# Down chunks in two halves between gate chunks, and weight loads of two chunks at a time, in a mixture-of-experts layer

## The chip, the cores and the metric

One core of one Trainium2 chip. The time is device microseconds of one execution. A core has TensorE (PE in the profile; PEld its weight loads), VectorE (DVE), ScalarE (ACT), GpSimd (POOL) and SyncE (SP). SyncE, ScalarE and GpSimd issue transfers, which run on 16 DMA engines. The kernel moves 450 MB, nearly all of it expert weights in float32.

## The reference, cut to what matters

512 tokens of width 1024 pass a layer with attention and a convolution, then a mixture of 32 experts, of which each token takes four. The expert part is what the change is about:

```python
def expert_block(args):
    tok, g, e = args
    xb = xf[tok]
    hu = xb @ w_gate_up[e] + b_gate_up[e]
    a = jnp.minimum(hu[:, :D_FF], SWIGLU_LIMIT)
    lin = jnp.clip(hu[:, D_FF:], -SWIGLU_LIMIT, SWIGLU_LIMIT)
    act = a * jax.nn.sigmoid(SWIGLU_ALPHA * a) * (lin + 1)
    return (act @ w_down[e] + b_down[e]) * g[:, None].astype(xb.dtype)
```

Here w_gate_up is (32, 1024, 2048) and w_down (32, 1024, 1024).

## The kernel before

The first 260 us compute the layer up to the router. Then the experts follow one after the other; one expert with up to 96 of its tokens is a job. Were an expert chosen by more than 96 tokens, further rounds of 32 jobs would follow; the number of jobs is read from memory (`bodies`, line 377). Jobs 0 and 1 are written out, and the rest is a hardware loop on each engine, with one job per pass.

A job's weights are 12 chunks of 1 MB, each 128 partitions by 8 KB: eight gate chunks (w_gate_up) and four down chunks (w_down). The chunks are numbered in the order in which PE uses them. `gu_chunk` (line 313) and `dn_chunk` (317) give the numbers, and `raw_slot` (298) gives the place in SBUF: 12 slots, chunk m in slot m % 12. Chunks 7 and 8 go to a place of their own once (`place`, 307). Before the change the twelve numbers of a job run: eight gates of expert j, then the four downs of expert j - 1.

SyncE issues the loads in this order (`job`, line 477), all on one queue. Each waits until the chunk 12 before it is used (`wait_slot`, 448): w_used counts the chunks that PE has finished, and chunk m waits for m - 11. Each slot has a semaphore w_loaded, on which PE waits ahead of the chunk.

On PE (`rest_of_job`, 1884, and `head`, 1873) a pass of the loop takes gates 4 to 7 of job j, the four downs of expert j - 1, and gates 0 to 3 of job j + 1. `gate_up` (1823) is 12 matmuls of 512 columns, four at a time side by side in the array; each is two instructions, with a weight load each. `down` (1834) is 24 matmuls of 256 columns in the same manner. So a gate chunk has 24 matmul instructions, a down chunk 48 of half the length. The gates of all jobs add up in the same banks gu_bank; gate 0 of the next job waits until VectorE has taken the sums (gu_taken) and has the next tokens ready (x_gained). The first down waits for the transposed activations (aT_ready) and for the down sums before it to be taken (y_taken).

On VectorE a job (`job`, 1529) takes the gate sums with the biases (lines 1461, 1462), clamps them (1465, 1466), transposes the gathered tokens of the next job (1472) and multiplies by the gain (1478), gates (1485, 1490, with ScalarE's sigmoid between), transposes the activations into aT (1498; chunk by chunk, each when its down chunk of the expert before is done), and takes the down sums (1511 to 1517). GpSimd gathers the tokens of the next job once x_turned tells that their place is free (line 651), and scatters the results, scaled by ScalarE, with addition into sum_rows (661). ScalarE loads the biases.

At the end PE takes the last expert's four downs by themselves, the last expert's rows are added by a matmul, and the final norm follows.

## Time and profile before

| | |
|---|---|
| Median of 3 runs (lowest, highest) | 1281.37 us (1281.32, 1281.72) |
| The profiled execution | 1282.38 us |
| Its span in the profile | 1280.6 us |
| Experts' part, from the first gate chunk | 262 to 1263 us |
| PE busy in the span | 1265.1 us |
| Moved by DMA | 450.31 MB |

The profile is of one execution. Busy time is the time in which an engine had an instruction at work; for PE the ends of matmuls are modelled. Times in the rows below are microseconds from the span's start, durations of one instruction in ns where three values stand with slashes (least, median, most). "Idle before" is followed by what ended it; "issue" means that the profile shows nothing for which the engine waited. In the chain, a piece is the stretch by which the end was advanced, not the whole length of an instruction. A DMA share is the busy share of the 16 engines; it can come out a little over 1.

### The profile page before, as it was taken

Reading aid. Unit: us, or ns where it says so; the run is one execution under the profiler, and the core shown is the slowest. Engines: PE = TensorE matmul, PEld = TensorE weight load, DVE = VectorE, ACT = ScalarE, POOL = GpSimd, SP = SyncE. Lnnn points to the kernel's source line nnn. Section 1 sums busy time; section 2 is a strip of 40 time slices with the busy share of each in tenths; the row PEclk is TensorE's granted clock in tenths of the full one; section 3 lists DMA queues with packets and bytes.
Section 4 is the critical chain, followed back from the end, with each engine's and each line's share of the span. In section 5 each row is a group of like instructions: output and inputs, shape, how many; then the busy total and the mean of one; then the engine's idle time right before and its main releaser. Section 6 shows DMA issues by size and latency. Waiting matters only on the chain.

```text
span 1280.6 us, 32819 instructions
## 1 busy us (share of the span) xinstructions
PE 1265.1 (99%) x13814; PEld 846.1 (66%) x13814; DVE 585.0 (46%) x984; ACT 184.2 (14%) x279; POOL 317.4 (25%) x319
## 2 busy tenths in 40 slices
PE   8999999999999999999999999999999999999997
PEld 7867777844676766766666556656576666667664
DVE  7776666555433333333333333333333333444345
ACT  4243443410000000000000000000000000000002
POOL 2035533011333332222222222222222222222220
PEclk9999999999999999999999999999999999999999
DMA  9222117589999999999999999999999999999994
GB/s 261 73 66 66 66 67 269 237 325 406 411 414 413 410 419 418 417 420 412 412 416 414 414 416 421 416 419 418 422 420 416 419 418 416 419 418 416 417 398 169
DMA packets 95377, 450.31 MB, mean 352 GB/s; under 512 B 12208, under 2 KB 37280, under 8 KB 45936
## 3 DMA queue, kind: packets, MB, share of 16 engines
q1 hardware_dynamic: 84288, 430.47, 82.2%
q0 software_dynamic: 9568, 18.97, 5.7%
q10 hardware_dynamic: 1488, 0.40, 0.1%
q8 instruction: 24, 0.39, 0.1%
q14 instruction: 9, 0.07, 0.0%
HBM read 439.54 MB, written 18.67 MB: 358 GB/s over the span
## 4 chain that ended last, share of the span: by engine, by line
PE 96%; DVE 2%; ACT 1%; DMA 1%; issue 0%; DVEq 0%; SPq 0%; ACTq 0%
PE gu_bank L1830 50%; PE bank L1844 21%; PE bank L1847 5%; PE bank L1597 5%; PE bank L1599 4%; PE bank L1598 4%; PE first_gu_bank L1830 2%; PE bank L1681 1%; PE bank L1695 1%; PE bank L1658 1%; DMA x_sb<-in_x_dram 1%; PE bank L1806 1%; DVE probs_a L1192 0%; PE fin_bank L1915 0%; PE bank L1615 0%
## 5 line engine op out<-in xcount | busy, mean ns | idle before, releaser
L1830 PE MATMUL gu_bank<-raw,xT 128*32 128x512 f32 x2976 | 331.7, 592 | 0.0
L1830 PEld LDWEIGHTS gu_bank<-raw,xT 128*32 128x32 f32 x2976 | 189.4, 110 | 130.4 <-issue 39.6
L1461 DVE TENSOR_TENSOR gate_in<-gu_bank,b_gu 128x768 f32<-128x768 f32 x31 | 29.7, 958 | 528.6 <-PE gu_bank L1830 528.6
L651 POOL DMA_INDIRECT x_got<-xn_rows,gather_list x96 | 114.5, 1193 | 341.7 <-DVE xT L1472 308.4
L1830 PE MATMUL gu_bank<-raw_c,xT 128*32 128x512 f32 x1488 | 172.1, 592 | 0.0
L1844 PE MATMUL bank<-raw_a,aT 128*32 128x256 f32 x2232 | 170.5, 379 | 0.0
L1847 PE MATMUL bank<-raw_a,aT 128*32 128x256 f32 x744 | 165.6, 379 | 0.0
L1844 PEld LDWEIGHTS bank<-raw_a,aT 128*32 128x32 f32 x2232 | 119.8, 110 | 36.5 <-issue 2.8
L1830 PEld LDWEIGHTS gu_bank<-raw_c,xT 128*32 128x32 f32 x1488 | 94.9, 110 | 65.2 <-issue 19.8
L937 ACT ACTIVATE sig_in<-gate_in 128x768 f32<-128x768 f32 x32 | 27.0, 845 | 641.0 <-DVE gate_in L1465 615.9
L1844 PE MATMUL bank<-raw_b,aT 128*32 128x256 f32 x1152 | 98.4, 380 | 0.0
L1847 PE MATMUL bank<-raw_b,aT 128*32 128x256 f32 x384 | 93.0, 380 | 0.1
L1830 PE MATMUL gu_bank<-raw_e,xT 128*32 128x512 f32 x744 | 92.3, 592 | 0.0
L1844 PE MATMUL bank<-raw_d,aT 128*32 128x256 f32 x1116 | 90.2, 379 | 0.0
L661 POOL DMA_INDIRECT sum_rows<-y_out,scatter_list x31 | 46.6, 1503 | 174.0 <-ACT y_out L945 114.2
L1830 PE MATMUL gu_bank<-raw_b,xT 128*32 128x512 f32 x720 | 89.5, 592 | 0.0
L1498 DVE STREAM_TRANSPOSE aT<-lin_in 128x192 f32<-128x192 f32 x128 | 63.6, 521 | 53.7 <-PE bank L1847 52.4
L1847 PEld LDWEIGHTS bank<-raw_a,aT 128*32 128x32 f32 x744 | 81.8, 110 | 7.1 <-issue 0.2
L1847 PE MATMUL bank<-raw_d,aT 128*32 128x256 f32 x372 | 85.3, 379 | 0.0
L945 ACT ACTIVATE y_out<-y_out,scatter_list 96x768 f32<-96x768 f32 (+1 forms) x62 | 44.8, 723 | 279.9 <-DVE y_out L1514 269.3
L1844 PEld LDWEIGHTS bank<-raw_b,aT 128*32 128x32 f32 x1152 | 62.0, 110 | 20.5 <-issue 6.0
L1844 PEld LDWEIGHTS bank<-raw_d,aT 128*32 128x32 f32 x1116 | 60.0, 110 | 15.0
(285 smaller groups left out, 1667.2 us busy)
## 6 DMA issues: line engine op xcount, KB each, us to landing
raw<-in_w_gate_up_dram SPq DMA_DIRECT2D x128, 1024.0 KB
raw_c<-in_w_gate_up_dram SPq DMA_DIRECT2D x62, 1024.0 KB
raw_a<-in_w_down_dram SPq DMA_DIRECT2D x62, 1024.0 KB
raw_b<-in_w_down_dram SPq DMA_DIRECT2D x32, 1024.0 KB
raw_e<-in_w_gate_up_dram SPq DMA_DIRECT2D x31, 1024.0 KB
raw_d<-in_w_down_dram SPq DMA_DIRECT2D x31, 1024.0 KB
raw_b<-in_w_gate_up_dram SPq DMA_DIRECT2D x30, 1024.0 KB
raw<-in_w_in_dram SPq DMA_DIRECT2D x24, 512.0 KB, 6.1
```

The source lines that it names most:

```text
L651: pool.indirect_dma_start(out=x_got[:, r, :], out_offset=None, in_=xn_quarters, in_offset=bass.IndirectOffsetOnAxis(ap=gather_list[:, r:r ...
L661: pool.indirect_dma_start(out=sum_rows, in_=y_out[0:TILE, :], in_offset=None, out_offset=bass.IndirectOffsetOnAxis(ap=scatter_list[0:TILE, ...
L937: act.activation(sig_in[:, :, :], gate_in[:, :, :], ACT.Sigmoid, scale=ALPHA).then_inc(sig_ready, 1)
L945: ins = act.activation(y_out[0:TILE, cols], y_out[0:TILE, cols], ACT.Copy, scale=scatter_list[0:TILE, 1:2].bitcast(F32))
L1461: dve.tensor_tensor(gate_in[:, :, :], gu[:, :, 0:QUARTER], gate_b, ALU.add)
L1498: dve.transpose(aT[:, 2 * i:2 * i + 2, :].rearrange("p k (r t) -> p k r t", r=GROUPS), lin_in[:, :, :].rearrange("p r (f k) -> p k r f", k ...
L1597: pe.matmul(dst, a_hi, b_hi, start=start, stop=False)
L1598: pe.matmul(dst, a_hi, b_lo, start=False, stop=False)
L1599: return pe.matmul(dst, a_lo, b_hi, start=False, stop=stop)
L1830: ins = pe.matmul(gu[c * GROUP:(c + 1) * GROUP, r, :], x[:, i, r * GROUP:(r + 1) * GROUP], w[:, c], start=first, stop=last)
L1844: pe.matmul(bank_[c * GROUP:(c + 1) * GROUP, cols], aT[:, k, c * GROUP:(c + 1) * GROUP], w[:, at:at + QUARTER], start=first and r % 2 == 0 ...
L1847: ins = pe.matmul(bank_[TILE:P, cols], aT[:, k, r * GROUP:(r + 1) * GROUP], w[:, at:at + QUARTER], start=first and r % 2 == 0, stop=last a ...
```

## The change

On PE the four downs stand in two halves: gates 4 and 5, downs 0 and 1, gates 6 and 7, downs 2 and 3, then gates 0 to 3 of the next job. The numbers of the chunks follow that (GU_AT, DN_AT). In the last job all four gates come first, then the four downs, while the numbers and SyncE's order stay as in the others.

The slots are ordered so that five times two of them lie side by side. SyncE loads ten of the twelve chunks of a job two at a time, 16 KB a partition with one semaphore; the source is contiguous for each partition. The load waits until both slots are free, and PE waits for it ahead of the first of the two alone. Job 0 and the four downs of the last expert are loaded one by one, and so are gates 0 and 1 of each job (slots 8 and 9).

On VectorE the clamps now follow the transpose and the gain of the next job's tokens. The last job is written out without that transpose and gain.

```diff
         def raw_slot(m):
 
-            for ring in (raw01, raw_a, raw_d, raw_b, raw_e, raw_c):
+            return raw_slots(m, 1)
+
+        def raw_slots(m, n):
+
+            for ring in (raw01, raw_a, raw_b, raw_d, raw_e, raw_c):
                 if m < ring.shape[1]:
-                    return ring[:, m, :]
+                    return ring[:, m:m + n, :].rearrange("p two n -> p (two n)")
                 m -= ring.shape[1]
 
-        ONCE = 7
+        TWO_AT = (0, 2, 4, 6, 10)
+
+        def starts_two(m):
+            return m >= RAW and m % RAW in TWO_AT
+
+        def ends_two(m):
+            return m >= RAW and m % RAW - 1 in TWO_AT
+
+        ONCE = 6
+        HEAD = GU_CHUNKS // 2
...
+        GU_AT, DN_AT = (0, 1, 2, 3, 4, 5, 8, 9), (6, 7, 10, 11)
+
         def gu_chunk(n, i):
 
-            return i if n == 0 else n * JOB - DN_CHUNKS + i
+            return i if n == 0 else n * JOB - DN_CHUNKS + GU_AT[i]
 
         def dn_chunk(n, i):
 
-            return n * JOB + 2 * GU_CHUNKS + i
+            return (n + 1) * JOB - DN_CHUNKS + DN_AT[i]
...
             def load_gu(e, i, m, b, turns):
-                wait_slot(m, b, turns)
-                sp.dma_start(place(m), w_gate_up[0, e].rearrange("(p i) n -> i p n", i=GU_CHUNKS)[i])\
+                if ends_two(m):
+                    return
+                n = 2 if starts_two(m) else 1
+                wait_slot(m + n - 1, b, turns)
+                sp.dma_start(raw_slots(m % RAW, n) if m >= RAW else place(m),
+                             w_gate_up[0, e].rearrange("(p i) n -> p (i n)", p=P)[:, i * CHUNK:(i + n) * CHUNK])\
                   .then_inc(w_loaded[m % RAW], 16)
 
-            def load_dn(e, i, m, b, turns):
-                wait_slot(m, b, turns)
-                sp.dma_start(raw_slot(m % RAW),
-                             w_down[0, e].rearrange("(p i h) n -> i p (h n)", p=P, i=DN_CHUNKS)[i])\
+            def load_dn(e, i, m, b, turns, n=1):
+                wait_slot(m + n - 1, b, turns)
+                sp.dma_start(raw_slots(m % RAW, n),
+                             w_down[0, e].rearrange("(p r) n -> p (r n)", p=P)[:, i * CHUNK:(i + n) * CHUNK])\
                   .then_inc(w_loaded[m % RAW], 16)
...
-                for i in range(first, GU_CHUNKS):
+                for i in range(first, HEAD):
                     load_gu(e, i, gu_chunk(n, i), b, turns)
-                for i in range(DN_CHUNKS):
-                    load_dn(before_e, i, dn_chunk(n - 1, i), b, turns)
+                for half in range(2):
+                    for i in range(HEAD + 2 * half, HEAD + 2 * half + 2):
+                        load_gu(e, i, gu_chunk(n, i), b, turns)
+                    load_dn(before_e, 2 * half, dn_chunk(n - 1, 2 * half), b, turns, 2)
...
-            for m in (0, 1, 4, 5, 6, 9, 7, 8, 2, 3):
+            for m in (0, 1, 4, 5, 8, 9, 6, 7, 2, 3):
                 load_early(m)
...
-            def clamp(j, used):
+            def take_gu(j, used):
...
                 dve.tensor_tensor(lin_in[:, :, :], gu[:, :, QUARTER:2 * QUARTER], lin_b, ALU.add)\
                    .then_inc(gu_taken, 1)
+
+            def clamp(j):
+
                 dve.wait_ge(gu_taken, j + 1)
...
-                clamp(j, later(gu_chunk(n, GU_CHUNKS - 1) + 1, b, BODY * JOB))
+                take_gu(j, later(gu_chunk(n, GU_CHUNKS - 1) + 1, b, BODY * JOB))
                 turn_got(j + 1, gathered)
                 gain_got(turned)
+                clamp(j)
                 gate(j)
                 turn_act(j, done)
                 take_y(j - 1, done[-1])
 
+            def last_job(n, b):
...
+                take_gu(j, later(gu_chunk(n, 0) + GU_CHUNKS, b, BODY * JOB))
+                clamp(j)
+                gate(j)
+                turn_act(j, done)
+                take_y(j - 1, done[-1])
...
             def gate_up(m, i, loads, gu=gu_bank, x=xT):
-                pe.wait_ge(w_loaded[m % RAW], loads)
+                if not ends_two(m):
+                    pe.wait_ge(w_loaded[m % RAW], loads)
...
+            def two_gates(n, first, turns):
+                for i in range(first, first + 2):
                     m = gu_chunk(n, i)
                     gate_up(m, i, turns[m // RAW])
-                pe.wait_ge(aT_ready, fixed(pe, j * DN_CHUNKS))
-                if n > 1:
-                    pe.wait_ge(y_taken, j - 1)
-                for i in range(DN_CHUNKS):
+
+            def two_downs(n, first, j, turns):
+                if first == 0:
+                    pe.wait_ge(aT_ready, fixed(pe, j * DN_CHUNKS))
+                    if n > 1:
+                        pe.wait_ge(y_taken, j - 1)
+                for i in range(first, first + 2):
                     m = dn_chunk(n - 1, i)
                     down(m, i, turns[m // RAW])
+
+            def rest_of_job(n, j, turns):
+                two_gates(n, HEAD, turns)
+                two_downs(n, 0, j, turns)
+                two_gates(n, HEAD + 2, turns)
+                two_downs(n, 2, j, turns)
+
+            def rest_of_last_job(n, j, turns):
+                two_gates(n, HEAD, turns)
+                two_gates(n, HEAD + 2, turns)
+                two_downs(n, 0, j, turns)
+                two_downs(n, 2, j, turns)
```

## Rows read from the trace of the kernel before

**Rows 1.** the page, part 1: busy time, share of the span, instructions

```profile
PE 1265.1 (99%) x13814; PEld 846.1 (66%) x13814; DVE 585.0 (46%) x984; ACT 184.2 (14%) x279; POOL 317.4 (25%) x319
```

**Rows 2.** busy time by stretch; PE, PEld, DVE, ACT, POOL, PEclk, DMA share, GB/s

```profile
350.00:700.00 350.00, 349.97 (x4298) 237.83 (x4293) 135.66 (x216) 26.61 (x35) 93.72 (x105) 1.00 1.02 416
...
234.00:236.00 2.00, 2.00 (x10) 1.62 (x9) 0.00 (x0) 0.00 (x0) 0.00 (x0) 1.00 0.10 41
```

**Rows 3.** timeline of DVE, line 1461, five of 31 starts

```profile
307.26 0.96 DVE L1461 TENSOR_TENSOR gate_in<-gu_bank,b_gu 128x768 f32<-128x768 f32 x1 [13.17 <-PE gu_bank L1830]
...
338.85 0.96 DVE L1461 TENSOR_TENSOR gate_in<-gu_bank,b_gu 128x768 f32<-128x768 f32 x1 [17.18 <-PE gu_bank L1830]
...
432.37 0.96 DVE L1461 TENSOR_TENSOR gate_in<-gu_bank,b_gu 128x768 f32<-128x768 f32 x1 [17.18 <-PE gu_bank L1830]
...
463.33 0.96 DVE L1461 TENSOR_TENSOR gate_in<-gu_bank,b_gu 128x768 f32<-128x768 f32 x1 [17.18 <-PE gu_bank L1830]
...
1243.20 0.96 DVE L1461 TENSOR_TENSOR gate_in<-gu_bank,b_gu 128x768 f32<-128x768 f32 x1 [17.19 <-PE gu_bank L1830]
```

**Rows 4.** the chain, one expert (start us, us, what)

```profile
681.33 0.22 PE bank L1844 x3
...
691.06 0.20 PE bank L1844 x2
...
691.28 0.40 PE bank L1847
...
692.12 20.60 PE gu_bank L1830 x192
```

**Rows 5.** timeline of weight loads at the same place

```profile
691.28 0.11 PEld L1847 LDWEIGHTS bank<-raw_b,aT 128*32 128x32 f32 x1 [0.51 <-issue]
```

**Rows 6.** timeline of SyncE's queue, before the experts and at the end

```profile
217.99 11.41 SPq L435 DMA_DIRECT2D raw<-in_w_gate_up_dram  x2
...
1235.46 2.04 SPq L520 DMA_DIRECT2D g_fin_row<-in_final_norm_g_dram  x1
```

**Rows 7.** tile g_fin_row

```profile
DMA to landing us min/median/max: 24.3/24.3/24.3
```

**Rows 8.** line 1844, the last two down chunks

```profile
L1844 PE MATMUL bank<-raw_c,aT x72: 379/379/379, 1258.2 to 1263.3; 128*32 128x256 f32 x72
```

**Rows 9.** line 439, loads into raw_c, 880 to 1000 and 1120 to 1240 us

```profile
L439 SPq DMA_DIRECT2D raw_c<-in_w_gate_up_dram x8: 332/332/333, 887.0 to 983.2; - x8
...
L439 SPq DMA_DIRECT2D raw_c<-in_w_gate_up_dram x6: 333/836/2288, 1136.6 to 1201.7; - x6
```

**Rows 10.** timeline after the gates of one expert

```profile
712.36 0.41 PE L1844 MATMUL bank<-raw_a,aT 128*32 128x256 f32 x3
...
712.89 0.96 DVE L1461 TENSOR_TENSOR gate_in<-gu_bank,b_gu 128x768 f32<-128x768 f32 x1 [17.18 <-PE gu_bank L1830]
713.76 0.95 DVE L1462 TENSOR_TENSOR lin_in<-gu_bank,b_gu 128x768 f32<-128x768 f32 x1
...
715.69 1.61 DVE L1472 STREAM_TRANSPOSE xT<-x_got 128x768 f32<-128x768 f32 x1
717.33 0.96 DVE L1478 TENSOR_TENSOR xT<-xT,g_ffn 128x768 f32<-128x768 f32 x1
...
720.19 1.46 DVE L1498 STREAM_TRANSPOSE aT<-lin_in 128x192 f32<-128x192 f32 x3
```

**Rows 11.** timeline of the final product, DVE to PE

```profile
1263.79 0.69 DVE L1511 TENSOR_TENSOR y_last<-bank,b_dn 96x512 f32<-96x512 f32 x1 [3.59 <-PE bank L1847]
...
1264.62 1.10 PE L1915 MATMUL fin_bank<-y_last,last_pick 96*128 96x512 f32 x2 [0.87 <-DVE y_last L1511]
```

**Rows 12.** DMA issues: count, KB each, median us to landing

```profile
sum_rows<-y_out,scatter_list POOLq DMA_INDIRECT x31, 8.4
```

**Rows 13.** DMA queue 1 in 700 to 900 and 240 to 252 us: packets, MB, share

```profile
q1 hardware_dynamic: 10956, 79.77, 94.6%
...
q1 hardware_dynamic: 699, 2.60, 53.5%
```

More of the change, by code:

```diff
@@ L463, in wait_slot @@
                     sp.wait_ge(scores_taken, HEADS * TT)
-                elif m == RAW_FRONT + 2:
+                elif m == ONCE + 2:
                     sp.wait_ge(lists_emptied, 16)
@@ L521, in _ @@
             stored = fixed(sp, later((FIRST - 1) * 16, count, BODY * 16))
-            used = fixed(sp, later(gu_chunk(FIRST - 1, GU_CHUNKS - 1) + 1, count, BODY * JOB))
+            used = fixed(sp, later(dn_chunk(FIRST - 2, DN_CHUNKS - 1) + 1, count, BODY * JOB))
             sp.wait_ge(y_stored, stored)
@@ L1524, in _ @@
             gain_got(1)
-            clamp(0, GU_CHUNKS)
+            take_gu(0, GU_CHUNKS)
+            clamp(0)
             gate(0)
@@ L1535, in job @@
                 gathered, turned = fixed(dve, j * 16 * GROUPS + 16 * GROUPS), fixed(dve, j + 1)
-                clamp(j, later(gu_chunk(n, GU_CHUNKS - 1) + 1, b, BODY * JOB))
+                take_gu(j, later(gu_chunk(n, GU_CHUNKS - 1) + 1, b, BODY * JOB))
                 turn_got(j + 1, gathered)
                 gain_got(turned)
+                clamp(j)
[3 more added lines that the diff above has]
+            def last_job(n, b):
+                j = job_no(dve, n, b)
+                gu_loads = fixed(dve, j * 16 + 16)
+                dve.wait_ge(b_gu_loaded, gu_loads)
+                done = [fixed(dve, later(gu_chunk(n, 0) + GU_CHUNKS + i + 1, b, BODY * JOB)) for i in range(DN_CHUNKS)]
+                spread_gu()
+                take_gu(j, later(gu_chunk(n, 0) + GU_CHUNKS, b, BODY * JOB))
+                clamp(j)
                 gate(j)
@@ L1544, in _ @@
             count = bodies(dve)
-            with dve.Fori(0, count) as b:
-                for n in range(FIRST, FIRST + BODY):
-                    job(n, b)
+            whole = dve.snap(count - 1)
+            with dve.Fori(0, whole) as b:
+                job(FIRST, b)
+            last_job(FIRST, whole)
             end = fixed(dve, later(FIRST, count, BODY))
@@ L1834, in down @@
             def down(m, i, loads, first_bank=4):
-                pe.wait_ge(w_loaded[m % RAW], loads)
+                if not ends_two(m) or first_bank != 4:
+                    pe.wait_ge(w_loaded[m % RAW], loads)
                 w = raw_slot(m % RAW)
@@ L1869, in _ @@
                     sum_lists()
-            HEAD = GU_CHUNKS // 2
             def head(n, j, turns):
@@ L1882, in head @@
                     gate_up(m, i, turns[m // RAW])
-            def rest_of_job(n, j, turns):
-                for i in range(HEAD, GU_CHUNKS):
+            def two_gates(n, first, turns):
+                for i in range(first, first + 2):
                     m = gu_chunk(n, i)
                     gate_up(m, i, turns[m // RAW])
-                pe.wait_ge(aT_ready, fixed(pe, j * DN_CHUNKS))
-                if n > 1:
-                    pe.wait_ge(y_taken, j - 1)
-                for i in range(DN_CHUNKS):
+            def two_downs(n, first, j, turns):
[4 more added lines that the diff above has]
+                for i in range(first, first + 2):
                     m = dn_chunk(n - 1, i)
                     down(m, i, turns[m // RAW])
+            def rest_of_job(n, j, turns):
[8 more added lines that the diff above has]
+                two_downs(n, 2, j, turns)
             assert BODY == 1
@@ L1904, in _ @@
                 head(FIRST + 1, fixed(pe, j + 1), turns)
-            rest_of_job(FIRST, job_no(pe, FIRST, whole), turns_of(pe, whole))
+            rest_of_last_job(FIRST, job_no(pe, FIRST, whole), turns_of(pe, whole))
             turns = turns_of(pe, count)
@@ L1909, in _ @@
                 pe.wait_ge(aT_ready, fixed(pe, later((FIRST - 1) * DN_CHUNKS + i + 1, count, BODY * DN_CHUNKS)))
-                down(m, i, turns[m // RAW], 6)
+                down(m, i, 32 if ends_two(m) else turns[m // RAW], 6)
             taken = fixed(pe, later(FIRST, count, BODY))
```

## The prediction

> **What bounds the kernel now.** I read the page first, then the busy time by stretch, the starts of one VectorE instruction per expert, the chain inside one expert, and last the DMA. PE is busy 1265.1 of 1280.6 us [rows 1], and between 350 and 700 us it is busy 349.97 of 350.00 us at a granted clock of 1.00, while the DMA engines show a share of 1.02 at 416 GB/s [rows 2]. The reader is to see that both are full at once: PE sets the time, and DMA has nothing to spare.
>
> The adds of line 1461 start once per expert, at 307.26 and finally at 1243.20 us [rows 3]; 30 periods lie between, so 31.20 us each. The first is 31.59 us (307.26 to 338.85), and one is 30.96 us (432.37 to 463.33). Eight gate chunks take 20.60 us, and four down chunks take 692.12 - 681.33 = 10.79 us in that job [rows 4]. A group of four down matmul instructions starts every 0.216 us (the chain advances by 0.20 and 0.01 us), and 48 groups would be 10.36 us; 20.60 + 10.36 = 30.96 us is the best job. What is lost stands near the end of the downs: at 691.06 the chain steps to 691.28 and stays there 0.40 us [rows 4], and the weight load at 691.28 was idle 0.51 us before it with no releaser ("issue") [rows 5]. The place is 9.95 us after the first down matmul, some 46 groups of 48; Such a piece stands at this place in nearly every job. A down group has as many instructions as a gate group (one takes 20.60/48 = 0.43 us) in half the time, so PE's sequencer falls behind during four downs, the queue of ready instructions runs empty, and there is one hole of some 0.2 us.
>
> The DMA side is tighter than it looks. The last early load goes out at the end of a piece that starts at 217.99 and lasts 11.41 us, at 229.4 us [rows 6], and from 234 us the engines are all but idle, share 0.10 [rows 2]: a chunk lands some 5 us after its issue. At the end, g_fin_row is issued at 1235.46 [rows 6] and lands 24.3 us later, at 1259.8 [rows 7]. It is 4 KB for each partition and right behind the last weight chunk, so that chunk lands at about 1258.5 on the slowest engine; PE uses it from about 1263.3 - 2.5 = 1260.8 us [rows 8]. So the slack of the slowest engine shrank from 28.4 - 5 = 23 us (a slot is reloaded 11 chunks ahead, 11 x 2.58) to some 2.3 us in 30 jobs, 0.7 us a job: that engine needs about 31.9 us a job where PE needs 31.2. SyncE agrees: its load instructions took 333 ns up to 983 us and up to 2288 ns after 1136 us [rows 9], which I read as a full queue.
>
> **The change part by part.** *PE order.* Nothing is added to PE's matmuls. Two downs (24 groups, 5.18 us) now stand between gates, and two gates take 5.15 us for half the instructions. In the four downs the reserve lasted 46 groups; after 24 it is half used, and the gates refill it. I take the hole as gone: per job 31.20 to 30.96. Its bounds are 0 (it stays) and 0.24 us a job. The TensorE page of the Trainium skill ("TensorE: Matmul & The Clock Gate", Specifications and Part 2) gives a queue of 64 and about 62 ns of sequencer time a MATMUL; against 54 ns that a down pair takes here, 182 pairs would lose an estimated 1.5 us, some 27 pairs of 32. The trace has no row of the sequencer's own time.
>
> *The new wait.* The next job's gate 0 now comes 5.18 us after the first down matmul, not 10.36. It waits for the scaled activations. DVE is moved to serve it first: adds, transpose, gain, then the clamps. From [rows 10]: downs from 712.36, line 1461 at 712.89, line 1462 at 713.76. The transpose can follow at 714.63 (one 0.87 us step), the gain 1.64 later at 716.27, done at 717.23. DVE to PE takes 0.14 us (1264.48 to 1264.62) [rows 11], so 717.37, and gate 0 is due at 712.36 + 5.18 = 717.54. It just fits; its weight load would like 717.32. I charge 0.05 us a job; bounds 0 and 0.25 (one more DVE step and an emptied queue). Behind that wait stand PE's gates 0 to 5 and so the w_used counts that SyncE's loads wait for.
>
> *What else moves on DVE.* Clamps, sigmoid and gating slip by 2.6 us and are followed by the four transposes; in the job shown the transposes of aT start at 720.19 [rows 10], 7.3 us after the gates' end, so aT is done within 10 us of it, and the downs that read it start 5.18 + 6 x 2.58 = 20.6 us after it. y_taken, 3 us later still, is needed at the same place. Cost nothing; if that cover of some 8 us went, downs 0 would be late. GpSimd's gather starts 1 us earlier, and the scatter's landing (8.4 us, [rows 12]) has 20 us of room, even if each of its rows waits behind a weight row of twice the length.
>
> *Loads by two.* A chunk is 8 rows (one per partition) on each of the 16 engines. The 96 rows of 8 KB of a job become 40 of 16 KB and 16 of 8 KB, 40 fewer. Prices from [rows 13]: in 700 to 900 us the queue moved 79.77 MB in 94.6% of 16 x 200 us, 26.35 GB/s, so 311 ns per 8 KB; in 240 to 252 us 2.60 MB in 53.5% of 16 x 12 us, 25.3 GB/s, so 162 ns per 4 KB. The straight line through both has 13 ns per row that does not grow with its size. 40 rows fewer save 0.52 us a job. Bounds: 0 (a 16 KB row is cut into two) and 0.52; I take 0.4, the upper one less the few stray long packets in the short window. The "DMA: Bandwidth & Descriptors" page of the Trainium skill (Why small descriptors are slow) speaks against it: about 3 bus cycles of 850 MHz a packet, 3.5 ns; by it the saving would be an estimated 0.14 us a job and the time about 1282. The rows here say more.
>
> Against that, the first chunk of a pair needs all 2 MB and its load waits until the second slot is free: one chunk, 2.6 us of slack, once. PE's faster job takes 0.2 us of slack each. So the slowest engine starts with 23 - 2.6 = 20.4 us and loses 0.7 + 0.2 - 0.4 = 0.5 us a job: 5.4 us are left after 30. In the last job PE takes gates 6 and 7 before downs 0 and 1, but SyncE loads them after: 5.2 us earlier than in the loop. 0.2 us is left, so I charge 0.5 us for it. SyncE issues fewer DMAs (seven a job, not twelve) and blocks less; it ends nothing.
>
> *Last job.* Four downs in a row remain there and four after it, as before: one hole stays, tail unchanged.
>
> **Sum.** First job -0.6; 30 jobs x (0.24 - 0.05) = -5.7; last job +0.5: -5.8 us. The profiled execution took 1282.38 us for a span of 1280.6; the median of the runs is 1281.37, 1.0 lower. 1282.38 - 5.8 = 1276.6 against its own time, and 1275.6 us on the scale of the median.
>
> **The rivals.** (1) *PE starves for weights, slower.* If the longer rows save nothing, slack falls by 0.9 a job: 20.4 - 27 - 5.2 = -12 us. PE waits that much, first for gates 2 to 5 late in the loop and most in the last job: -6.3 + 12 = +5.7, 1287. It decides once the saving is under 0.25 us a job (time even with before) and begins at 0.4. For it: the shrinking slack and the full queue [rows 7, 9]. Against: the two prices per row [rows 13]. At 0.14 us a job it gives 1283. (2) *The hole moves.* The wait for the activations comes 0.2 us later than I worked out and PE's queue is empty there: one hole per job again, 1281. For it: 0.2 us of room. (3) *The hole is tied to something else* (the instruction stream's refill, or each phase of downs): it stays, 1281, or comes twice, 1287. The page "Runtime: NRT & Kernel Launch" of the Trainium skill (Instruction fetch mechanics) has refills every 256 instructions and a stall at a taken branch; by that alone the hole would stay. Against: the first job, outside the loop, has the hole too, 31.59 us, and it stands at one place of the phase. (4) The change not taking hold: the loads are still one by one on the wire, which is (1).
>
> **How the numbers follow.** My forecast has 0.60, and lies between 1273.6 (no hole, no new wait, DMA in time: -7.8) and 1278.5. Rival 1 has 0.20: 0.10 at 1283 to 1287 and 0.10 in part, 1279 to 1283. Rival 2 has 0.10 and rival 3 0.10, of it 0.03 twice. What a measurement here can tell from no change is 0.2%, 2.6 us: 1278.8 to 1283.9. Faster 0.66, same 0.21, slower 0.13. The range from 1273.2 to 1283.5 leaves out the slow ends.
>
> **What would show it.** Right: starts of the adds after the gates 30.96 to 31.05 us apart; no "issue" idle before line 1844's weight loads; two blocks of 5.2 us of downs a job; q1 with 16 KB rows at over 26.5 GB/s for its busy share; g_fin_row landing no later after issue than 24 us. Wrong: PE waiting at gate 0 on DVE (rival 2), PE idle before lines 1830 or 1844 ended by a DMA after some 900 us or in the last job (rival 1), or holes unchanged in number (rival 3).

## The result and the profile after

In the first comparison the changed kernel took 1287.24 us (median of 5 runs, 1285.79 to 1288.82), the kernel before 1281.32: ratio 1.005, interval 1.0039 to 1.0061. On another chip it was 1.008, interval 1.0063 to 1.0097. It is slower by 6 to 10 us where 5.8 us less was forecast. (Of the runs below, `pairs_only` had one execution of 2212.23 us, which is left out of its ratio.) The profiled execution took 1286.82 us for a span of 1285.1.

First the timeline of VectorE after the change, the adds that stood at line 1461 and stand at 1482 (answers to [rows 3]):

```profile
311.35 0.96 DVE L1482 TENSOR_TENSOR gate_in<-gu_bank,b_gu 128x768 f32<-128x768 f32 x1 [17.62 <-PE gu_bank L1870]
...
342.39 0.96 DVE L1482 TENSOR_TENSOR gate_in<-gu_bank,b_gu 128x768 f32<-128x768 f32 x1 [16.98 <-PE gu_bank L1870]
...
930.63 0.96 DVE L1482 TENSOR_TENSOR gate_in<-gu_bank,b_gu 128x768 f32<-128x768 f32 x1 [18.32 <-PE gu_bank L1870]
...
961.59 0.96 DVE L1482 TENSOR_TENSOR gate_in<-gu_bank,b_gu 128x768 f32<-128x768 f32 x1 [18.26 <-PE gu_bank L1870]
...
992.80 0.96 DVE L1482 TENSOR_TENSOR gate_in<-gu_bank,b_gu 128x768 f32<-128x768 f32 x1 [18.20 <-PE gu_bank L1870]
...
1214.02 0.96 DVE L1482 TENSOR_TENSOR gate_in<-gu_bank,b_gu 128x768 f32<-128x768 f32 x1 [18.85 <-PE gu_bank L1870]
...
1247.66 0.96 DVE L1482 TENSOR_TENSOR gate_in<-gu_bank,b_gu 128x768 f32<-128x768 f32 x1 [20.90 <-PE gu_bank L1870]
```

From 311.35 to 342.39 are 31.04 us, then every period is 30.96 up to 961.59. In this execution the hole is gone, at the size that was forecast. From there the jobs lengthen, 31.21 to 992.80 and then 31.4 to 32.0: over the eight loop jobs to 1214.02, 252.43 us instead of 8 x 30.96 = 247.68, a loss of 4.75. The last period is 33.64, where two downs and eight gates in a row allow 25.78 (10 x 2.58): a loss of 7.86. Together 12.6 us.

Who is waited for shows in the waits of PE from 900 us on (engine, line, what was waited for: us in total, times, longest), and in the chain of the last job (start us, us, what):

```profile
PE gu_bank L1870 <- DMA raw_a<-in_w_gate_up_dram: 4.8, 1, 4.8
PE bank L1885 <- DMA raw<-in_w_down_dram: 2.9, 7, 0.8
```

```profile
1208.67 5.18 PE gu_bank L1870 x48
1214.02 25.19 DMA raw_a<-in_w_gate_up_dram
1239.25 8.20 PE gu_bank L1870 x48
```

The waits shown on PE itself in the loop are for down weights (raw), 2.9 of the 4.75 us; its weight loads wait for DMA there too, which the profile lists apart, so the rest is not divided up. The last job's is one wait of 4.8 us for the pair of gates 6 and 7 (raw_a). It was issued at 1214.02, as its slots came free, and landed 25.19 us later. And the 48 groups of two gates, 5.18 us in the job before, take 8.20 us after the wait. The windows of the same stretch (columns as in [rows 2]) show the clock:

```profile
1230.00:1234.00 4.00, 4.00 (x44) 1.37 (x36) 0.00 (x0) 0.00 (x0) 1.30 (x1) 1.00 1.01 360
1234.00:1240.00 6.00, 1.21 (x11) 0.20 (x8) 0.00 (x0) 0.00 (x0) 0.18 (x1) 0.85 0.99 410
1240.00:1244.00 4.00, 4.00 (x24) 0.99 (x20) 0.00 (x0) 0.00 (x0) 0.00 (x0) 0.50 0.62 259
1244.00:1250.00 6.00, 6.00 (x80) 2.36 (x76) 2.31 (x4) 0.00 (x0) 0.00 (x0) 0.91 0.25 106
```

PE is busy 1.21 of the 6 us to 1240. The granted clock falls to 0.50, the lower of the two levels (1.2 GHz), at about 1238.2, within the wait, and is back at 1.00 at about 1245. A wait of 4.8 us costs 7.9, since 3.0 us of slow gates come behind it.

The weights' way there is seen best in the time from issue to landing of the pair in raw_a (both gates 6 and 7), in four windows: 320 to 352, 470 to 502, 930 to 962, 1060 to 1092 us:

```profile
DMA to landing us min/median/max: 10.9/10.9/10.9
...
DMA to landing us min/median/max: 14.2/14.2/14.2
...
DMA to landing us min/median/max: 24.8/25.2/25.6
...
DMA to landing us min/median/max: 25.7/25.7/25.7
```

A pair can be 25.7 us under way; then PE waits for it. The second loop job's needed 10.9 already, so 14.8 us of slack were there, not the 20.4 of the forecast. By 962 us, 20 jobs later, it was 25.6: 0.73 us lost a job, not 0.5. What the pairs are worth shows in queue 1 from 700 to 900 us (packets, MB, share; answer to [rows 13]), after the change and then in a kernel with the new order and single loads:

```profile
q1 hardware_dynamic: 6527, 80.40, 94.3%
```

```profile
q1 hardware_dynamic: 10938, 79.64, 94.4%
```

80.40 MB in 94.3% of 16 x 200 us are 26.64 GB/s per engine; 79.64 MB in 94.4% are 26.36, as before. So 16 KB take 615 ns against 621.5 for two rows of 8 KB, and the 40 merged rows save an engine some 0.27 us a job, not 0.4.

### The profile page after: what moved, and what is told of

It is laid out like the page before. It is cut to its first block, busy times and chain, and to the rows that moved or that the text cites. A ratio compares the mean times of both kernels' runs of the same rounds, so it can differ in the third digit from the quotient of the medians.

```text
span 1285.1 us, 32211 instructions
## 1 busy us (share of the span) xinstructions
PE 1262.5 (98%) x13814; PEld 677.1 (53%) x13814; DVE 577.2 (45%) x982; ACT 184.1 (14%) x279; POOL 320.9 (25%) x319
## 3 DMA queue, kind: packets, MB, share of 16 engines
q10 hardware_dynamic: 1488, 0.40, 0.1%
## 4 chain that ended last, share of the span: by engine, by line
PE 78%; DMA 17%; DVE 3%; issue 1%; ACT 1%; POOL 0%; SPq 0%; DVEq 0%; POOLq 0%; ACTq 0%
PE gu_bank L1870 38%; PE bank L1885 22%; DMA raw<-in_w_down_dram 14%; PE bank L1636 5%; PE bank L1638 4%; PE bank L1637 4%; DMA raw_a<-in_w_gate_up_dram 2%; PE bank L1720 1%; PE bank L1734 1%; PE bank L1697 1%; PE bank L1888 1%; DMA x_sb<-in_x_dram 1%; PE bank L1845 1%; DMA x_got<-xn_rows,gather_list 0%; PE first_gu_bank L1870 0%
## 5 line engine op out<-in xcount | busy, mean ns | idle before, releaser
L1870 PE MATMUL gu_bank<-raw_a,xT 128*32 128x512 f32 x1488 | 169.0, 601 | 4.8 <-DMA raw_a<-in_w_gate_up_dram 4.8
L1885 PE MATMUL bank<-raw,aT 128*32 128x256 f32 x2232 | 166.8, 379 | 2.9 <-DMA raw<-in_w_down_dram 2.9
L1885 PE MATMUL bank<-raw_b,aT 128*32 128x256 f32 x2232 | 166.8, 379 | 0.0
L1870 PE MATMUL gu_bank<-raw,xT 128*32 128x512 f32 x1488 | 166.1, 592 | 0.0
L1888 PE MATMUL bank<-raw,aT 128*32 128x256 f32 x744 | 165.8, 379 | 0.0
L1888 PE MATMUL bank<-raw_b,aT 128*32 128x256 f32 x744 | 165.6, 379 | 0.0
L1885 PEld LDWEIGHTS bank<-raw,aT 128*32 128x32 f32 x2232 | 110.0, 110 | 63.3 <-issue 22.3
L1885 PEld LDWEIGHTS bank<-raw_b,aT 128*32 128x32 f32 x2232 | 109.6, 110 | 58.9 <-issue 14.0
L1870 PEld LDWEIGHTS gu_bank<-raw,xT 128*32 128x32 f32 x1488 | 57.5, 110 | 102.1 <-issue 97.9
L1870 PEld LDWEIGHTS gu_bank<-raw_a,xT 128*32 128x32 f32 x1488 | 57.3, 111 | 97.8 <-issue 87.6
L1870 PE MATMUL gu_bank<-raw_d,xT 128*32 128x512 f32 x744 | 86.3, 592 | 0.3 <-DVE xT L1502 0.3
L1888 PEld LDWEIGHTS bank<-raw_b,aT 128*32 128x32 f32 x744 | 82.0, 110 | 0.0
L1888 PEld LDWEIGHTS bank<-raw,aT 128*32 128x32 f32 x744 | 81.3, 110 | 0.0
L1636 PE MATMUL bank<-xnT_hi,hi 128*128 128x512 f32 x160 | 66.6, 416 | 1.0 <-DVE xnT_lo L1140 1.0
```

The source lines that it names most:

```text
L1636: pe.matmul(dst, a_hi, b_hi, start=start, stop=False)
L1870: ins = pe.matmul(gu[c * GROUP:(c + 1) * GROUP, r, :], x[:, i, r * GROUP:(r + 1) * GROUP], w[:, c], start=first, stop=last)
L1885: pe.matmul(bank_[c * GROUP:(c + 1) * GROUP, cols], aT[:, k, c * GROUP:(c + 1) * GROUP], w[:, at:at + QUARTER], start=first and r % 2 == 0 ...
L1888: ins = pe.matmul(bank_[TILE:P, cols], aT[:, k, r * GROUP:(r + 1) * GROUP], w[:, at:at + QUARTER], start=first and r % 2 == 0, stop=last a ...
```

## The experiments

Eighteen runs on five chips, each beside the kernel before on the same chip; five of them repeat a kernel as it was. "Period" is the distance between two of VectorE's adds as above.

### First chip: the weights' arrival taken away

before 1282.13 us (25 runs). `light_before`, `light_after`: of slot 9's chunk only a quarter is loaded, so they do not compute the layer (the diff is that of the second).

```diff
+                few = CHUNK // 4 if m >= RAW and m % RAW == 9 else n * CHUNK
+                dst = raw_slots(m % RAW, n) if m >= RAW else place(m)
+                sp.dma_start(dst[:, 0:few],
```

> The kernel before, with one weight load of the twelve of a job (slot 9) cut to 512 of its 2048 columns, so that gate chunk 1 of each later expert computes with mostly old columns. DMA per job falls by 0.79 of 12.58 MB, so the slowest engine needs about 31.9 x 0.94 = 30 us a job and is never late. Theory (the hole of 0.2 us is PE's own sequencer falling behind in four downs): time unchanged, 1281 us, periods of 31.2 us stay. Rival (the hole comes from the full DMA engines, by fetches or late weights): periods fall to 30.96 us and the time to about 1274 us.

1280.61 us, ratio 0.9992 (0.9982 to 1.0002). The holes stay (most periods 31.15 to 31.20, 31.19 on average) with lighter transfers, so they are no waits for weights.

> The changed kernel with the same cut of slot 9's load (gate chunk 1 computes with mostly old columns). Theory (the changed kernel lost only by late weights): every period 30.96 us, none of PE's waits ended by a DMA, 1287.2 less 4.7 us in the last loop passes and 7.9 us in the last job, so 1274.6 us. Rival (something of the new order costs by itself, such as the last job or the wait at gate 0): above 1278 us.

1284.09 us, ratio 1.0018 (1.0008 to 1.0028); a miss by 9.5. The late loss is gone (30.96 from 475 us on, last job 25.78, no wait of PE for a DMA), but four early periods are 33.23, 33.15, 33.10 and 33.21 us. A loss that the profile of the changed kernel didn't have. PE's timeline in the first of them, in downs 0 and 1, and GpSimd's at the same time:

```profile
334.41 0.42 PE L1887 MATMUL bank<-raw,aT 128*32 128x256 f32 x3
334.68 0.38 PE L1890 MATMUL bank<-raw,aT 128*32 128x256 f32 x1
334.70 1.13 PE L1887 MATMUL bank<-raw,aT 128*32 128x256 f32 x6
335.46 0.39 PE L1890 MATMUL bank<-raw,aT 128*32 128x256 f32 x1
335.48 0.40 PE L1887 MATMUL bank<-raw,aT 128*32 128x256 f32 x1
...
337.67 0.44 PE L1887 MATMUL bank<-raw,aT 128*32 128x256 f32 x3 [0.34 <-issue]
```

```profile
331.86 1.05 POOL L710 DMA_INDIRECT lists<-entry,dest  x1 [0.58 <-issue]
...
335.81 0.98 POOL L710 DMA_INDIRECT lists<-entry,dest  x1 [0.31 <-issue]
```

A group of four should start every 0.216 us. From 334.68 to 337.67 most take 0.5 to 0.8 us, with no releaser; then the pace is back. The job lost 33.23 - 31.04 = 2.2 us. Beside it, from 331.86 to 336.79, GpSimd issues four indirect DMAs of its overflow list (first and last shown), as in each of these four jobs and no other. That the two belong together is not shown by this run.

`light_clampfirst`: `light_after` with VectorE's old order (clamps first).

```diff
-                turn_got(j + 1, gathered)
-                gain_got(turned)
                 clamp(j)
+                turn_got(j + 1, gathered)
+                gain_got(turned)
```

> As light_after (same cut), but VectorE clamps before the transpose and the gain of the next tokens, as in the kernel before. The scaled tokens come 0.94 us later, at 718.3 on the scale of the prediction where gate 0 is due at 717.54 and they were there at 717.37. Theory: PE waits 0.8 to 0.95 us at gate 0 in each of 30 jobs, 24 to 28 us more than light_after, about 1299 us. Rival (PE's queue or a shorter chain hides it): under 5 us more.

1303.93 us, ratio 1.0172 (1.0155 to 1.0189); 19.8 us more than `light_after`, where 24 to 28 were expected. The loop's period is 31.68, 0.72 over 30.96. So the new wait has no room for the clamps, and with VectorE's new order the undisturbed periods of 30.96 leave nothing for it.

`last_order`: the changed kernel, with SyncE's loads of the last job in PE's order.

```diff
+                if last:
+                    for i in range(HEAD, GU_CHUNKS):
+                        load_gu(e, i, gu_chunk(n, i), b, turns)
+                    for i in (0, 2):
+                        load_dn(before_e, i, dn_chunk(n - 1, i), b, turns, 2)
+                    return
```

> The changed kernel, but in the last job SyncE loads gates 6 and 7 before downs 0 and 1, in the order in which PE takes them there. Theory: gates 6 and 7 land 5.2 us earlier on the slowest engine, at 1234.0 where PE is ready at 1233.9, so the wait of 4.8 us goes and with it the half clock behind it (some 3 us): 1287.2 - 7.9 = 1279.3 us. Rival (the last job is late by lack of slack, not by order): under 3 us gained, 1284 us or more.

1285.08 us, ratio 1.0021 (1.0012 to 1.0031); a miss by 5.8 in time, though not in mechanism. The last period is 25.78: the 7.9 us are had back. But this profile has the early loss as well (33.30, 33.05, 32.33, 32.33, 32.33 us), which hides part of it. The fifth of these jobs has no store: its downs 0 and 1 slow down from 467 us, while GpSimd issues the next tokens' three gathers and the scatter in a row (463.50 to 469.2 us). The same windows as above, of the same kernel on the fifth chip (`last_order_b`), show PE busy throughout and no low clock:

```profile
1234.00:1240.00 6.00, 6.00 (x60) 2.21 (x56) 0.00 (x0) 0.00 (x0) 1.30 (x1) 1.00 1.00 372
1240.00:1244.00 4.00, 4.00 (x41) 1.42 (x36) 0.00 (x0) 0.00 (x0) 0.18 (x1) 1.00 1.01 422
```

### Second chip: the early loss and GpSimd's stores

before 1280.44 us (31 runs). One wait on GpSimd moves the four stores of a job beside gates 6 and 7 (in `stores_before`, where they stood beside gates, it moves them beside the four downs, by `gu_chunk(n, GU_CHUNKS - 1) + 1`).

```diff
                     part = TT * TOPK // PEELED
+                    pool.wait_ge(w_used, dn_chunk(n - 1, 1) + 1)
```

> Leaves out three quarters of the chunk in weight slot 9 of every expert, as the earlier run with the lightened load did, and adds one wait on GpSimd: in its four jobs with stores of the overflow list (16 indirect DMAs in all) the stores wait until TensorE is through downs 0 and 1, so that they fall beside gates 6 and 7. Theory: TensorE's instruction queue is refilled more slowly while GpSimd issues indirect DMAs; beside the 128-row gate matmuls (107 ns each) that is hidden, beside the downs (54 ns each) it is not, and it made the 2.2 us in each of four jobs (33.1 to 33.2 us instead of 30.96). Then these four periods become 31.0 and the time falls from 1284.1 by about 8.8 to 1275.3 (1274.5 to 1276.5). Rival: the loss belongs to TensorE's own first passes through its loop, or to the DMA queues in that stretch: the periods stay at 33 wherever GpSimd's stores lie, 1284.

1278.3 us (1275.57 to 1282.86), ratio 0.9989 (0.9973 to 1.0005): between the two forecasts. The early periods are 31.04 and 30.96; the sixth is 33.88, a loss of 2.9 us. It is the new wait at gate 0. GpSimd's gathers of the next tokens go out at 462.53 to 465.39 us and take up to 7.7 us to land; VectorE, done with its adds, waits for them, and gate 0 comes only behind its transpose and gain:

```profile
473.15 1.55 DVE L1499 STREAM_TRANSPOSE xT<-x_got 128x768 f32<-128x768 f32 x1 [3.24 <-DMA x_got<-xn_rows,gather_list]
...
475.80 1.50 PE L1873 MATMUL gu_bank<-raw_d,xT 128*32 128x512 f32 x12 [2.72 <-issue]
```

The downs before it ran at full pace up to 472.7 us. No run in the new order on this chip has its stores beside the downs, so whether the early loss would have come here is not known.

> The kernel before with one wait added on GpSimd, which moves the same four groups of four stores from beside the gates into the stretch of the four downs in a row. Theory (GpSimd's indirect DMAs slow the supply of TensorE's instructions): a pair of weight load and matmul then takes about 90 ns instead of 66 for the 5.2 us of the stores, 58 pairs x 24 ns = 1.4 us in each of four jobs and more if the queue is empty sooner, so 5 to 9 us slower, 1286 to 1290. Rival (the first passes of TensorE's loop, or the DMA queues): no change, 1281 to 1282.

1280.57 us, ratio 1.0001 (0.9992 to 1.0011): stores beside the downs cost nothing here, and the hole of 0.2 us a job was gone too. Against the theory; and the time was the same, since eight late periods of 31.2 to 32.1 took the holes' place.

> The changed kernel, whole computation, with the last job's weights asked for in the order in which TensorE uses them there, and with GpSimd's stores moved beside gates 6 and 7. Theory: the early loss (8.9 us in the profile of the run with the last job's order alone) goes, but it had given the weight transfers time; without it TensorE catches up with the slowest DMA engine as in the changed kernel, 4.75 us in the loop, and only the last job's 7.9 us are saved: 1286.8 - 7.9 = 1279 (1277.5 to 1281). If the transfers did not matter there: 1274.6.

1279.82 us, ratio 0.9996 (0.9986 to 1.0005): no early loss, last period 25.78, as expected. The late jobs are 31.1 to 32.0; eleven of them lose 6.1 us where 4.75 were expected.

`best`: `last_stores`, and the down bias (4 KB, one row) loaded by an access pattern of 16 pieces.

> As the run before it, and the load of the down bias, which today is one row of 4 KB and so lies on a single DMA engine, is split into 16 pieces, one for each engine. Theory: this engine is the one that lags behind the others by some 5 us (24 to 26 us from issue to landing, the next ones 20); 31 x 0.16 us = 5 us of its work is spread, so TensorE does not catch up with it before the end: all loop periods 30.96, last job 25.8, 1274.6 to 1276.5, faster than both kernels. Rival: the slowest engine is slow for another reason, then it is as the run before it, 1279.

1279.48 us, ratio 0.9993 (0.9983 to 1.0003), every late period within 0.03 us of `last_stores`. The edit did nothing: queue 10, which carries the biases, has as many packets in the one as in the other (first `best`, then `last_stores`), where 16 pieces would have made 15 x 31 more. It tells nothing on that row.

```profile
q10 hardware_dynamic: 1488, 0.40, 0.1%
```

```profile
q10 hardware_dynamic: 1488, 0.40, 0.1%
```

### Third chip: is it the kernel or the chip?

before 1279.7 us (9 runs). `placebo_light` and `placebo_before` have the same instruction on GpSimd, waiting for something long past; the other two are unchanged repeats.

```diff
+                    pool.wait_ge(w_used, 1)
```

> The kernel with the lightened slot 9 (three quarters of that chunk left out) and the same added GpSimd instruction as in the run that moved the stores, but waiting for something long past (the first weight chunk used), so that the stores stay where they were, beside downs 0 and 1. Theory (the four indirect stores beside the downs cost TensorE's supply of instructions 2.2 us a job): the early periods stay at about 33 us and the time at 1284 (1282.9 to 1286). Rival (it is not where the stores lie in time, but how GpSimd's program is laid out, since one instruction was added): the early periods become 31.0, 1275 to 1279, as in the run that moved them.

1275.16 us, ratio 0.9966 (0.9954 to 0.9979), and no early loss: the number of the rival. But `light_after_again` below shows that this chip has no early loss without the added instruction either.

> The kernel before with that same instruction, waiting for something long past, so nothing moves in time. In the run that moved the stores beside the four downs the hole at their end (0.2 us a job) was gone, in the same time of the whole. If the hole goes here too, it is the layout of GpSimd's program or chance, not the stores' place; if it stays (periods 31.15 to 31.20), the place of the stores matters for all later jobs as well. Time 1280 to 1282 either way, since the weights' arrival takes the place of the hole.

1279.89 us (one execution), no hole.

> The kernel before, unchanged, one more profile: does the hole of 0.2 us a job come in each execution? If it belongs to the program, periods of 31.15 to 31.20 again; if it is a matter of the execution, some profile shows 30.96. Time 1280 to 1282.

1279.84 us (one execution), no hole. VectorE's timeline of this execution of the kernel before:

```profile
305.83 0.96 DVE L1461 TENSOR_TENSOR gate_in<-gu_bank,b_gu 128x768 f32<-128x768 f32 x1 [13.19 <-PE gu_bank L1830]
...
336.87 0.96 DVE L1461 TENSOR_TENSOR gate_in<-gu_bank,b_gu 128x768 f32<-128x768 f32 x1 [17.16 <-PE gu_bank L1830]
...
987.03 0.96 DVE L1461 TENSOR_TENSOR gate_in<-gu_bank,b_gu 128x768 f32<-128x768 f32 x1 [17.17 <-PE gu_bank L1830]
...
1018.48 0.96 DVE L1461 TENSOR_TENSOR gate_in<-gu_bank,b_gu 128x768 f32<-128x768 f32 x1 [17.66 <-PE gu_bank L1830]
...
1240.68 0.96 DVE L1461 TENSOR_TENSOR gate_in<-gu_bank,b_gu 128x768 f32<-128x768 f32 x1 [17.45 <-PE gu_bank L1830]
```

31.04 us to the second, then 21 of 30.96 up to 987.03, and 31.2 to 32.1 after it: the last eight take 253.65 us instead of 247.68, a loss of 6.0. SyncE's gate loads from 1000 to 1180 us (line 439; first those into raw_c, then the time to landing of all 48) show that the weights are late: the load instructions are held up, 1884 ns in the median, and a landing takes up to 29.1 us, more than the 28.4 us from issue to use:

```profile
L439 SPq DMA_DIRECT2D raw_c<-in_w_gate_up_dram x12: 332/1884/4568, 1006.3 to 1166.4; - x12
...
DMA to landing us min/median/max: 26.2/27.8/29.1
```

> The changed kernel with the lightened slot 9 (three quarters of that chunk left out), unchanged from the earlier run, one more profile: if the loss of 2.2 us in each of four early jobs belongs to the program, it is there again (four periods of 32.3 to 33.3) and the time is 1283 to 1286; if it is a matter of the execution, the periods are 31.0 in some.

1274.69 us, where the same kernel took 1284.09 on the first chip:

```profile
311.29 0.96 DVE L1484 TENSOR_TENSOR gate_in<-gu_bank,b_gu 128x768 f32<-128x768 f32 x1 [17.39 <-PE gu_bank L1872]
...
1209.21 0.96 DVE L1484 TENSOR_TENSOR gate_in<-gu_bank,b_gu 128x768 f32<-128x768 f32 x1 [18.20 <-PE gu_bank L1872]
...
1234.99 0.96 DVE L1484 TENSOR_TENSOR gate_in<-gu_bank,b_gu 128x768 f32<-128x768 f32 x1 [13.01 <-PE gu_bank L1872]
```

923.70 us from the first to the last are 31.04, 28 periods of 30.96 and one of 25.78, none lost. So neither the hole nor the early loss comes wherever its kernel runs; each depends on the chip or the execution as well. It depends on the kernel too: the early loss was seen in the new order alone, and no profile of the order before has it. 1274.7 is what the changed kernel would take if weights never came late and PE's instructions in time. The layout of GpSimd's program is not ruled out as a part of the early loss: on a chip without the loss the added instruction can tell nothing, and it was not tried on one that has it.

### Fourth chip: what each part is worth

before 1280.77 us (16 runs).

> The changed kernel, unchanged, on whichever chip this call gets; the runs so far show the loss of 2.2 us in each of four early jobs on one chip and not on two others, and the hole of the kernel before likewise. Theory: the end of both kernels is set by the weights' arrival, so neither the hole nor the early loss is in the time: before 1279.5 to 1281.5, this 1285.5 to 1288, with the last job's period at 33.6 (7.9 us over 25.78) and 4 to 7 us lost in late loop jobs. Rival (the time of the changed kernel in the first comparison came from the chip's own loss): then it is faster than before here, 1274 to 1278.

1290.8 us (1288.88 to 1292.26), ratio 1.008, above the 1285.5 to 1288 expected. Early periods 32.88, 32.66, 32.10, 31.90, 32.01 (6.8 us over 30.96), three late ones lengthened by 1.5 us in all, last one 33.24 (7.5 over 25.78): 15.7 us lost where the first profile lost 12.6. An early loss gives the transfers time, so about half of it takes the place of the late one (1.5 and 7.5 instead of 4.75 and 7.9); the other half is in the time, against the theory.

`pairs_only`: before's order on PE and SyncE, with the pairs and VectorE's new order. The expectation below has all twelve chunks in pairs; it is ten, since TWO_AT is unchanged and slots 8 and 9 (raw_d, raw_e) are still loaded one by one, 31 loads of 1 MB each.

```diff
-        GU_AT, DN_AT = (0, 1, 2, 3, 4, 5, 8, 9), (6, 7, 10, 11)
+        GU_AT, DN_AT = (0, 1, 2, 3, 4, 5, 6, 7), (8, 9, 10, 11)
...
                 two_gates(n, HEAD, turns)
-                two_downs(n, 0, j, turns)
                 two_gates(n, HEAD + 2, turns)
+                two_downs(n, 0, j, turns)
                 two_downs(n, 2, j, turns)
```

> The order of before on TensorE and SyncE (gates 4 to 7, then four downs), with the chunks loaded two at a time (all twelve, in six pairs) and VectorE's new order kept. Theory: the end goes by the slowest DMA engine; a pair saves it 0.2 us a job (31.87 to 31.66), some 6 us in 30 jobs, and a load that waits for two free slots instead of one starts later by up to one chunk, 2.6 us, which it must make good once; before loses 6.0 us to late weights in its last eight jobs where there is no hole. So 1276 to 1279.5. Rival (longer rows save the DMA engines nothing): 1280 to 1283, by the later start.

1279.39 us, ratio 0.999 (0.998 to 1.0); late jobs still lose 4.8 us. The four downs stand in a row and GpSimd's stores beside gates here, and there is neither a hole (periods of 30.96, two of 31.05) nor the early loss, on the chip that shows it in the new order just above and below.

`order_last`: the new order with single loads, last job's loads in PE's order (as in `last_order`).

> The changed order on TensorE (two halves of the downs) with single loads as before, and in the last job SyncE's loads in TensorE's order. Beside last_stores (the same with pairs, 1279.8) it shows what the pairs are worth. Theory (0.2 us a job on the slowest engine, 6 us in 30 jobs, less up to 2.6 us for the earlier issue of single loads): 1282 to 1286. Rival (pairs worth nothing): 1277 to 1280.

1284.16 us, ratio 1.0032 (1.0021 to 1.0044), beside 1.0021 and 1.0019 for the same with pairs on other chips. As expected. With the early loss in both, the difference would make the pairs worth about 1 to 2 us; the intervals overlap, so it is not shown.

### Fifth chip: the slowest DMA engine, and the stores again

before 1282.2 us (25 runs). `bdn_small`: of the down bias, all experts but the first load 32 bytes instead of 4 KB, so most of that bias is left out.

```diff
+                few = D_FF if isinstance(j, int) and j == 0 else 8
+                act.dma_start(b_dn[0:1, 0:few], b_down[0, bass.ds(fixed(act, expert(j)), 1), 0:few])\
```

> The kernel before with the down bias left out of all experts but the first: of its row of 4 KB, which lands as one packet on a single DMA engine, only the first 32 bytes are loaded. Theory (the end is set by the slowest DMA engine, and this row is what makes it slower than the others, 0.16 us a job of its own): without it some 30 x 0.16 = 4.8 us of the 6.0 us that before loses to late weights are saved where there is no hole, 1275.5 to 1278. Rival (that engine is slow for another reason, or the transfers as a whole set the end): 1279.5 to 1281, as before. Where the chip shows the hole of 0.2 us a job, less of it is visible: 1279 to 1281.

1282.2 us, ratio 1.0 (0.9991 to 1.001). This chip shows the hole (most periods 31.13 to 31.35), so nothing could come of it in the time. But beside the profile of the kernel before that the prediction rests on, which shows the hole as well, the transfers moved as the theory has it: raw_c's loads from 1000 to 1180 us never block SyncE, and g_fin_row lands after 21.8 us, not 24.3 [rows 7]:

```profile
L439 SPq DMA_DIRECT2D raw_c<-in_w_gate_up_dram x12: 332/333/333, 1011.5 to 1170.0; - x12
```

```profile
DMA to landing us min/median/max: 21.8/21.8/21.8
```

The trace holds 16 landings for each load, and those of g_fin_row agree: in the kernel before 15 lie between 1243.35 and 1254.82 us and the last by itself at 1259.78; without the row all 16 lie between 1241.67 and 1254.57. One of the 16 was 5 us behind the others, and it is the row that made it so. That it is worth 5 us where there is no hole was not seen.

> The changed kernel with the last job's loads in TensorE's order, once more, as the pair to the next run on the same chip. If this chip shows the early loss: four or five periods of 32.3 to 33.3 and 1283 to 1286; if not: 1278.5 to 1281.

1284.03 us (1282.78 to 1286.72), ratio 1.0019 (1.0009 to 1.0029). The early loss is there: 32.75, 33.07, 32.07, 32.25, 32.24 us, 7.6 over 30.96.

> The same with GpSimd's stores moved beside gates 6 and 7. If the stores beside the downs are what makes the early loss on the chips that have it, this one shows none (1278.5 to 1282) where the run before it does (1283 to 1286). If both have it, the stores are not its cause; if neither has it, this chip can't tell.

1280.26 us (1279.77 to 1281.5), ratio 0.9986 (0.9977 to 0.9996). Early periods 32.00, 31.51, 31.52, 31.47, 32.34: 4.0 over. On a chip that has the loss, moving the stores away from the downs takes back half of it, 3.8 us of the time; whether by their place or by the added instruction alone is not separated here. What remains is of two kinds. In the first four jobs the downs run at full pace, but VectorE's adds start later behind the gates: in the first job 1.37 us after the first down (342.48 to 343.85 us), where it is 0.75 later on (717.62 to 718.37), and gate 0 waits for the tokens that VectorE makes ready after them (gain from 347.21 to 348.17, gate 0 at 348.28). In the fifth the downs slow down at 463 us beside three gathers and a scatter. It is the one run of the whole computation that is faster than the kernel before outside its interval, by 1.8 us.

## Why the prediction was wrong

Two terms failed, and both are about the weights: the slack of the slowest DMA engine, which was put too high, so that the waits in the loop stood at nothing and cost 4.75 us; and the last job, charged 0.5 us, which cost 7.9.

**The hole.** Removed as forecast, 31.20 to 30.96 us. On the two chips where a kernel in the order before shows it (`light_before`, `bdn_small`), the new order's periods behind the early jobs are 30.96 as well. But it was not what alone set the end. Where a chip shows no hole, before takes 1279.8 us all the same, because the weights come late by 6.0 us in the last eight jobs. The two limits lie within 2 us of each other, and taking away the nearer one gives those 2 us, not 5.7. The runs agree: with the last job's loads in order and the stores moved, the kernel takes 0.6 us less than the kernel before on a chip without the hole, and 1.9 less on one with it. The sentence that PE sets the time was the trace's, but of one execution. The 62 ns that the prediction takes from the page "TensorE: Matmul & The Clock Gate" of the Trainium skill (Part 2) stand there for the case that hardware decode is off, a condition that no run here shows.

**The new wait.** Charged 0.05 us a job, measured nothing in the first comparison; the room that VectorE's new order makes for it is worth 0.72 a job. But it is as narrow as the prediction says: late gathers made it cost 2.9 us once (`light_stores`), and adds 0.6 us late 0.5 to 1.0 us a job in four (`last_stores_b`).

**The pairs.** 0.4 us a job was charged, some 0.27 measured in the packets' own time: the step that took "13 ns per row" from a short window was too large by a factor of two. The page "DMA: Bandwidth & Descriptors" of the Trainium skill (Why small descriptors are slow) gave an estimated 0.14; the measurement lies between it and the forecast.

**The slack at the start.** This is the first of the two terms that failed. The 20.4 us rested on "a chunk lands some 5 us after its issue"; the queues fill in the first loop jobs, and the second pair needed 10.9 us. With 14.8 us and 0.73 a job the end comes after 20 jobs, at the very place where the periods lengthen. Of the 0.23 us a job by which the slack shrank faster than forecast, 0.13 are the pairs' smaller saving.

**The last job.** The second. The 5.2 us by which PE comes earlier to gates 6 and 7 there was seen, but charged at 0.5 on top of slack that did not exist. It cost 4.8 us of waiting, and 3.0 more at half the clock, for which the sum had no term.

**The rivals.** Rival 1 is what happened, by its mechanism: PE starves for weights, late in the loop and most in the last job. That its sum agrees too, 12 us of waits and 1287 against 12.6 and 1287.24, is luck. Its condition, rows that save nothing, did not hold: with the measured 0.27 us a job its own working gives 20.4 - 18.9 - 5.2 = -3.7 us and about 1279. The slack at the start was lower than it has it, and 3.0 of the 12.6 us are the clock, which it does not have. (Its limit for a time even with before, a saving of 0.25, is by the same working 0.18.) 1274.7 (`light_after_again`) and 12.6 make 1287.3. Rival 2 did not come in the first comparison. Rival 3 did not come either. It was right only in that the order of the instructions alone does not make the hole, since it is missing in that order on the second, third and fourth chip; what the queue's emptying is tied to stays open.

**Open.** Why PE's instructions come more slowly in the new order on the first, fourth and fifth chip and not on the third, nor in the first comparison. GpSimd's indirect DMAs beside the downs are probably a part of it there: 3.8 us were had back by moving four of them a job, and the fifth job slows down beside others. Yet they cost nothing on the third chip, nor beside the four downs of the order before on the second. Open is also how much of the kernel before's loss the single row of the down bias explains.

## What to carry to other kernels

When two limits lie as close as here, price an edit against both: a faster engine only brings the next limit's moment forward. Read slack as the time to landing in several windows, from the profile's first loop jobs to its last, rather than from the two ends. Let the order of the loads follow the order of use in a peeled last job too, and before a removed stall is counted, see it in a second execution on another chip.

## What the runs showed of the hardware

The granted clock fell to 0.50 during a wait of TensorE of 4.8 us, some 3.8 us into it, and stayed there until 5.8 us behind it, which made the wait cost 1.6 times its length. One row of 4 KB a job was enough to put one of the last load's 16 landings 5 us behind the others, and to make that load take 2.5 us longer (24.3 against 21.8). An access pattern of 16 pieces over a contiguous row went out in as many packets as the row in one piece (1488 on the queue in both). And one and the same kernel (`light_after`) took 1284.09 us on one chip and 1274.69 on another, by the pace of TensorE's instructions where a group of four starts every 0.216 us, while the kernel before took 1279.7 to 1282.2 us on all five.
